# Branch merge of a hybrid attention block: seven half-size products for each pair of feature blocks, with sums on GpSimd and VectorE

## What is computed

```python
def merge_branches(o_mla, o_fox, o_mem, gates, w_br_mla, w_br_fox, w_br_mem, w_out):
    b, s = gates.shape[:2]
    y = (gates[:, :, 0] * (o_mla.reshape(b, s, -1) @ w_br_mla)
         + gates[:, :, 1] * (o_fox.reshape(b, s, -1) @ w_br_fox)
         + gates[:, :, 2] * (o_mem.reshape(b, s, -1) @ w_br_mem))
    return y @ w_out
```

## Time and profile before

| | |
|---|---|
| median of 3 runs | 1071.58 us (1070.4 to 1073.7) |
| profiled execution | 1072.0 us |
| its span, first to last instruction | 1069.8 us |
| granted TensorE clock, mean | 0.992 |
| PE busy | 1035.6 us (97%) |
| DVE busy | 597.4 us (56%) |
| ACT busy | 182.0 us (17%) |
| POOL busy | 94.7 us (9%) |

### The profile page before, as it was taken

One profiled execution on the slowest core, in us unless ns is written; L12 is line 12 of the kernel. 1 busy time (PEld: TensorE's weight loads), 2 busy tenths in 40 slices (PEclk: granted clock), 3 DMA queues, 4 the chain that ended last, 5 costly groups with the idle time before them and its releaser, 6 DMA issues.

```text
span 1069.8 us, 17897 instructions
## 1 busy us (share of the span) xinstructions
PE 1035.6 (97%) x6615; PEld 660.0 (62%) x6648; DVE 597.4 (56%) x1476; ACT 182.0 (17%) x365; POOL 94.7 (9%) x111
## 2 busy tenths in 40 slices
PE   8999999999999999998999999999999999999985
PEld 4499569989888755466655555555555555555541
DVE  2445047777666333366686655555655655654636
ACT  1411224443223100010001011011011101101102
POOL 4140000000000000002014410000000000000000
PEclk9999999999999999999999999999999999999988
DMA  9633443523767598561598999999999999999981
GB/s 335 220 117 105 131 145 112 203 95 115 280 216 248 188 335 323 245 221 43 217 412 336 406 413 419 421 420 418 420 417 412 422 420 421 421 420 419 407 346 61
DMA packets 82333, 313.56 MB, mean 293 GB/s; under 512 B 13208, under 2 KB 24016, under 8 KB 56024
## 3 DMA queue, kind: packets, MB, share of 16 engines
q1 hardware_dynamic: 64864, 276.90, 65.7%
q10 hardware_dynamic: 10128, 19.40, 5.0%
q0 software_dynamic: 7280, 16.44, 4.3%
HBM read 306.24 MB, written 11.34 MB: 297 GB/s over the span
## 4 chain that ended last, share of the span: by engine, by line
PE 93%; DVE 4%; DMA 2%; issue 1%; ACT 0%; SPq 0%; DVEq 0%
PE ps_P L1372 21%; PE ps_P L1120 16%; PE ps_V L1396 11%; PE ps_V L1360 8%; PE ps_V L1308 6%; PE ps_P L999 4%; PE ps_S L1360 4%; PE ps_V L1156 4%; PE ps_T L1354 3%; PE ps_T L992 2%; DMA arena<-w_e_gate 1%; PE ps_P L1008 1%; PE ps_P L1174 1%; PE ps_V L1342 1%; PE ps_S L1379 1%
## 5 line engine op out<-in xcount | busy, mean ns | idle before, releaser
L1372 PE MATMUL ps_P<-arena,branch_out 128*64 128x256 f32 (+1 forms) x2176 | 236.1, 385 | 4.7 <-DMA arena<-w_e_gate 3.9
L1372 PEld LDWEIGHTS ps_P<-arena,branch_out 128*64 128x64 f32 (+1 forms) x2176 | 153.2, 137 | 95.6 <-issue 25.7
L1396 PE MATMUL ps_V<-arena,branch_out 128*64 128x512 f32 (+1 forms) x544 | 120.6, 598 | 0.0
L1610 ACT ACTIVATE weight_ring<-ps_V,merge 128x512 f32<-128x512 f32 x66 | 45.3, 687 | 382.0 <-PE ps_V L1396 356.3
L1360 PE MATMUL ps_V<-weight_ring,branch_out 128*128 128x512 bf16 x363 | 93.7, 390 | 2.2
L2133 DVE TENSOR_TENSOR branch_out<-branch_out,ps_P 128x256 f32<-128x256 f32 x33 | 13.9, 421 | 143.5 <-PE ps_P L1372 143.4
L2160 DVE TENSOR_TENSOR x_sb<-x_sb,ps_V 128x512 f32<-128x512 f32 x132 | 87.4, 684 | 1.3 <-PE ps_V L1360 1.3
L2123 DVE TENSOR_TENSOR weight_ring<-weight_ring 128x512 f32<-128x512 f32 x64 | 44.4, 693 | 68.2 <-ACT weight_ring L1610 65.9
L1120 PE MATMUL ps_P<-xT,weight_ring 128*128 128x192 f32 x432 | 78.9, 327 | 0.8 <-ACT arena L1522 0.8
L1396 PEld LDWEIGHTS ps_V<-arena,branch_out 128*64 128x64 f32 (+1 forms) x544 | 34.8, 135 | 68.7 <-issue 68.6
L1120 PEld LDWEIGHTS ps_P<-xT,weight_ring 128*128 128x128 f32 x432 | 70.2, 190 | 3.3 <-issue 2.9
(11 more groups left out here) (360 smaller groups left out, 1250.8 us busy)
## 6 DMA issues: line engine op xcount, KB each, us to landing
arena<-w_e_gate SPq DMA_DIRECT2D x68, 1024.0 KB
arena<-w_e_up SPq DMA_DIRECT2D x68, 1024.0 KB
arena<-w_e_down SPq DMA_DIRECT2D x68, 1024.0 KB
weight_ring<-w_in SPq DMA_DIRECT2D x12, 1024.0 KB, 9.2
weight_ring<-w_in ACTq DMA_DIRECT2D x8, 1024.0 KB, 6.7
gates<-arena ACTq DMA_DIRECT2D x12, 384.0 KB, 3.1
arena<-fox_k_t SPq DMA_DIRECT2D x8, 512.0 KB, 3.8
arena<-cache_fox_v SPq DMA_DIRECT2D x8, 512.0 KB, 4.3
```

The lines of the kernel that those rows point to most:

```text
L1372: last = mm(bank[r:r + wide, 0:256], xgT[q][:, k, r:r + wide], w[h][:, k, :], start=(k == 0), stop=(k == KD - 1))
L1396: last = mm(ps["V"][half][r:r + wide, :], hidT[:, m, r:r + wide], ew_down[h][:, m, half * 512:(half + 1) * 512], start=(m == 0), stop=(m = ...
L1610: fn(yo[:, half * 512:(half + 1) * 512], ps["V"][half][:, :], ACT.Copy, scale=now_info[:, q, 1:2])\
```

## The change

The 24 entries of the merge become 12 units, u from 0 to 11, of the seven-product scheme that the gates already use. A unit takes a pair of feature blocks (m = 0 and 1, or 2 and 3) of one branch and one half cb, and splits the 512 features of `oT` into two halves of 256 and the 384 tokens into two of 192. A product is two matmuls on 192 columns in place of four, so that a unit has 14 matmuls where two entries had eight on 384 columns. The units are numbered on from the gates' units (`JOIN` = 18) and use the same two `ps_P` banks and the same semaphores.

- Sums of weights: three for each unit ahead of it (`sum_weights`) and one within it (a12), each 128 x 256, all on GpSimd.
- Sums of `oT`: four for each branch, 128 x 384 each, on VectorE (the entries `"mix"`). The four of branch 0 stand among the last entries of attention, the eight others behind products 2 and 4 of units 0 to 3.
- Sums of results: ScalarE copies product 0, VectorE adds the others, as in the gates' units.
- Gating: one VectorE multiplication of 128 x 768 in each unit (`gate_rows`), behind the last sum.
- Addition to `yT`: one of 128 x 768 on GpSimd (`join`) for the units of branches 1 and 2, a unit later.
- Gate tiles are loaded in pairs. The eight of the start come behind ScalarE's copy of product 0 of unit 0.
- The load of expert pair 1 also waits for the last addition to `yT`, since the new buffers lie in its place.

```diff
+    at = max(i for i, st in enumerate(s) if st[:2] == ("V", "ov")) + 1
+    for m in range(4):
+        s.insert(at + 3 * m, ("mix", 0, m))
+    sums = [("mix", br, m) for br in (1, 2) for m in range(4)]
+    for u in range(JOINS):
+        for r in range(7):
+            s.append(("W", JOIN + u, r))
+            if r in (2, 4) and sums:
+                s.append(sums.pop(0))
-    s += [("V", "b", cb, br, m) for cb, br, m in MERGE]
...
+            def sum_weights(u):
+                i = JOIN + u
+                a11, a12, a21, a22 = join_weights(u)
+                all_, less = join_sums(u)
+                n = first_of["br"] + u // 2
+                pool.wait_ge(w_loaded[n % NW], loads_of(n))
+                pool.wait_ge(done["W"], done_at("W", JOIN - 1 if u < 2 else i - 2, 4))
+                nc.gpsimd.tensor_tensor(all_, a21, a22, ALU.add).then_inc(w_mixed, 1)
+                pool.wait_ge(w_mixed, 4 * i + 1)
+                nc.gpsimd.tensor_tensor(less, all_, a11, ALU.subtract).then_inc(w_mixed, 1)
+                nc.gpsimd.tensor_tensor(a21, a11, a21, ALU.subtract).then_inc(w_mixed, 1)
+
+            def join(u):
+                cb, br, m = join_parts(u)
+                if br:
+                    pool.wait_ge(gated, u + 1)
+                    if br == 2:
+                        pool.wait_ge(merged, joined_at(cb, 1, m))
+                    nc.gpsimd.tensor_tensor(join_rows(u), join_rows(u), join_two[u % 2], ALU.add).then_inc(merged, 1)
+
+            sum_weights(0)
+            for u in range(JOINS):
...
+                pool.wait_ge(done["W"], done_at("W", i, 2))
+                pool.wait_ge(w_mixed, 4 * i + 3)
+                nc.gpsimd.tensor_tensor(a12, a12, join_sums(u)[1], ALU.subtract).then_inc(w_mixed, 1)
+                if u + 1 < JOINS:
+                    sum_weights(u + 1)
+                if u:
+                    join(u - 1)
+            join(JOINS - 1)
...
+                nk = 2 if i >= JOIN else 4
+                for k in range(nk):
+                    last = mm(gate_bank(i, r), w[:, k, :], x[:, k, :], start=(k == 0), stop=(k == nk - 1))
...
+                            act.wait_ge(done["W"], done_at(*st))
+                            fn(product_cells(i)[:, 0, 0:HALF], gate_bank(i, r), ACT.Copy).then_inc(w_copied, 1)
+                            if u == 0:
+                                make_gates(TWO - 1)
+                                while gates["stored"] < gates["made"]:
+                                    store_gates()
+                                for n in range(4, 4 + KD):
+                                    load_gate(n)
...
+            def gate_rows(u):
+                for n in (2 * u, 2 * u + 1):
+                    dve.wait_ge(gates_loaded[gate_buffer(n)], 16 * (1 if n < 4 else (n - 4) // KD + 1))
+                dve.wait_ge(w_read, 7 * (JOIN + u) + 7)
+                to = join_rows(u) if join_parts(u)[1] == 0 else join_two[u % 2]
+                V.tensor_tensor(to, join_two[u % 2], join_gates(u), ALU.mult).then_inc(gated, 1)
...
                     else:
                         dve.wait_ge(w_read, 7 * i + 5)
                         V.tensor_tensor(c12, out, c12, ALU.add).then_inc(w_read, 1)
+                        if i >= JOIN:
+                            gate_rows(i - JOIN)
...
+                    V.tensor_tensor(to, more, less, ALU.subtract).then_inc(o_mixed, 1)
```

More of the change, by code:

```diff
@@ L468, in build @@
         rs = M.take(len(U))
+        joining = Space(R_A, 18432, 12288)
+        o_mix = [[joining.take(2, HALF) for _ in range(4)] for _ in range(3)]
+        join_two = [joining.take(2, T) for _ in range(2)]
         egate = [v.rearrange("p m c -> p (m c)")[:, i * 512:i * 512 + T] for v in (fkTc[0], mkTc[0]) for i in range(2)] + [xT[:, k, :] for k in range(KD)]
```

136 lines of the change are left out of this document (87 added, 49 removed).

## The result

The changed kernel takes 1083.89 us (median of 4 runs, 1081.06 to 1084.77) against 1071.84 (1070.4 to 1073.7): ratio 1.0109, 95% interval 1.009 to 1.0129. It is 12.05 us slower; the forecast was 5.2. Its profiled execution took 1083.82 us, with a span of 1082.0 at a granted clock of 0.991.

What follows compares the result with a forecast made beforehand. PE was taken to bound the merge (62.19 of 62.20 us busy). Products 54.6, banks 5.8, burst 1.35, `oT` sums 0.2 and entry 0.47 make 62.4; serial engines add 5.0: 67.4 against 62.2, hence 1076.8 us, range 1068 to 1084.

Steps and rivals of the forecast that it cites:

- two banks: Merge products on PE: each bank comes back later than the other bank's product covers, 0.48 us a unit, 5.8 in all.
- ScalarE's burst: Start of the merge: eight gate loads ahead of unit 1's copy of product 0 delay product 2, 1.35 us once.
- sums of `oT`, held or not: VectorE in units 0 to 3: 0.2 us for too little room, 2.0 for meeting GpSimd's a12 in three units.
- gating against GpSimd's addition: Units with an addition to `yT`: gating and GpSimd's work run serially, +0.4 us in each of seven units, 2.8.
- GpSimd's price: GpSimd's additions in the merge: 2.1 ns a column, 0.64 and 1.71 us; 4.5 us a unit fits into 5.03.
- The lock: In the merge, VectorE operations with two SBUF inputs and GpSimd's additions run one after the other, 5.0 us in all.
- The entry: Before the merge's first product: a sum of `oT` ahead of VectorE's last copy moves that copy by 0.47 us.
- The exit: End of the merge: last gating and addition end about 3.4 us behind the last product, hidden before the output projection's need.
- The stage behind: The experts' stage moves as a whole with the merge's end, its first matmul staying 89.8 us behind.
- The third, GpSimd as the bound: Rival for the merge: at 2.5 to 3 ns a column GpSimd limits the units, 1082 to 1088 us; chance 0.12.
- The second, the bank in time: Rival for the merge: banks return below 0.65 us, only product 6's 0.27 stays, 1069.2 or 1066 us; chance 0.08.
- The first, no lock between additions: Rival for the merge: GpSimd's and VectorE's work lie side by side, +0.2 us, 1071.8 us; chance 0.32.

Runs made afterwards that it cites:

- e5: The changed kernel with the merge's products in four PSUM banks in turn instead of two: 1072.0 us, ratio to before 0.9993.
- e3: The changed kernel with GpSimd's additions to `yT` left out, so the output sums only branch 0: 1074.0 us (one run).
- e6: The changed kernel with ScalarE's eight gate loads issued as 2, 4 and 2 in the first three units: 1083.1 us (one run).
- e1: The changed kernel with three cell buffers instead of two for a unit's products: 1079.7 us, ratio to before 1.006.
- f2: As f1, but the addition to `yT` stays on GpSimd, ahead of the next unit's weight sums: 1077.8 us, ratio to before 1.0055.
- e8: The changed kernel with four banks and three cell buffers: 1071.5 us, ratio to before 0.999.
- e2: The changed kernel with GpSimd making the addition to `yT` ahead of the next unit's weight sums: 1081.1 us, ratio to before 1.0078.
- e4: The changed kernel with the weight sums on VectorE, GpSimd keeping only the additions to `yT`: 1079.9 us, ratio to before 1.0072.
- e7: The changed kernel with the addition to `yT` on VectorE, two banks and two cell buffers: 1082.5 us, ratio to before 1.0087.
- f1: The changed kernel with four banks, three cell buffers, gate loads spread and the addition to `yT` on VectorE: 1069.1 us, ratio to before 0.9966.
- f3: As f1, but with the changed kernel's two cell buffers: 1068.6 us, ratio to before 0.9962.
- f4: As f1, with two of the first branch's four `oT` sums moved behind attention's last copy: 1068.6 us, ratio to before 0.9963.

## Why the prediction was wrong, point by point

The direction held, and of the mechanisms two banks and one port. The size did not, and one mechanism was missing. By the prediction's own terms, with what the runs measured (apart from the products and the banks they are differences between kernels, so that their sum meets 70.9 by construction):

| term | predicted us | measured us | from |
|---|---|---|---|
| 84 products | 54.6 | 54.6 | e5, units of 4.55 |
| two banks | 5.8 | 7.8 | e3 and e5, 12 x (5.20 - 4.55) |
| ScalarE's burst | 1.35 | 0.7 | e6 |
| sums of `oT`, held or not | 0.2 + 2.0 | 2.2 | what is left of e3's 65.3 |
| gating against GpSimd's addition | 2.8 | 2.8 | e1 less e3 |
| some tenths for gating against weight sums | 0.2 | 0 | e3's timeline |
| the copy behind the addition of unit u-2 | not seen | 2.8 | changed less e1 |
| merge | 66.9, with the entry's 0.47 67.4 | 70.9, with the entry's 0.5 71.4 | |

**The step that failed** is in "GpSimd's price": "A unit with an addition to `yT` then has 4 x 0.64 + 1.71 = 4.3 us of GpSimd's, with 0.2 for its waits 4.5, and lasts 5.03. It fits." I compared a load with a period, and asked only whether the next unit's sums are ready. A load that fits says nothing of a circle. What GpSimd's last operation in the row gives free, the cell buffer, is asked for by ScalarE's copy, then product 2, and product 2 releases GpSimd's first. The circle is 6.12 us long, 4.7 in GpSimd's five operations (390.42 to 395.10) and 1.45 through the copy and product 2 (395.10 to 396.55), with every link of it known ahead: the prices were all but right. I had named who waits for the weight sums, and not who waits for the addition, except at the merge's exit. With the circle the additions cost 5.6 us (changed less e3), where the prediction had 2.8 for them.

**The two banks** were the second error, a size: 0.65 a unit and not 0.48. In the unit of e3 whose gating is shown above, products 1 to 5 start at 408.15, 408.87, 409.57, 410.30 and 410.95, and product 6 at 411.92; by 413.35, product 1 of the next unit, two more distances have passed. Less 0.65 each, that is 0.07, 0.05, 0.08, 0, 0.32, and 0.13 for the two. Product 6's 0.32 was foreseen at 0.34. The small losses, which I had at 0.07 in two places of a unit, 0.14 in all, come to 0.33, as the banks never get ahead again.

**GpSimd's price** was nearly right. The prediction took 0.64 and 1.71 us; alone, the changed kernel's operations take 0.72 and 1.81 (L981 and L990 above), which is 2.1 ns a column and 0.18 fixed: a load of 4.7 in place of 4.3. The Trainium skill ("GPSIMD Engine Reference", section Elementwise, side-by-side cycle accounting) has 4497 ns for 2048 columns, 2.2 each; by that alone 256 columns would be 0.56 and 768 1.7. The rows are above it by what is fixed.

**The lock** was there as forecast, and was the case that no row of before had shown. Two VectorE inputs in SBUF beside a GpSimd addition: the gating 0.96 alone and 1.95 behind an addition of 1.81; the sums of `oT` 0.55 and 0.91; GpSimd's sums 0.73 and 1.04. VectorE's additions with an input in PSUM stay at 0.34 to 0.36 beside the same work. By the rule of the Trainium skill ("SBUF — State Buffer", section Terms, and the reading of its diagram), whichever begins first keeps the port for its whole instruction; the trace agrees in both orders. What the rule does not tell is its price, which hangs on when the two meet: 2.8 us in e1, where an addition is late, and nothing for the gating in e3. That the 2.8 is also the forecast is luck. The prediction had seven units of 0.4 each, the two engines' work added up against PE's time; e1 has three units of 0.75 to 1.0 by a bank that comes back late, and three of 0.15. In the changed kernel itself the lock's share for the additions can't be told apart: the circle accounts for the whole of its units of 6.13, and the weight sums in them are not held (0.72).

**The sums of `oT`** were forecast at 0.65 in units 0, 2 and 3, hidden in unit 1, and 0.2 for VectorE's room. They cost about the same in another spread, some 0.5 in each of units 0 to 3: unit 1 lasts 5.67 without the burst (e6), units 2 and 3 5.73, against 5.20. How much of it is the lock and how much VectorE's own time no run separates.

**ScalarE's burst** had its mechanism right and its size double: unit 1 loses 0.7. The prediction's own figures, 8.1 less 6.6, give 1.5 and not 1.35. Counted from the merge's start, product 2 of unit 1 began at 7.7 in place of 8.1, and without the burst (e6) at 7.0 in place of 6.6, since unit 0 lasts 5.67 and not 5.03.

**The entry** was right: the sum of `oT` ahead of the last copy, a wait of 1.0 in place of 0.5, +0.5 against 0.47. **The exit** was right as well: the experts begin 524.2 - 434.4 = 89.8 us behind the merge's end, to the tenth as foreseen.

**The stage behind** did not just move. In the changed kernel PE waited there for a gather of rows, which the stage of before never did:

```profile
PE ps_T L1455 <- DMA weight_ring<-x_rows,idx: 3.4, 1, 3.4
...
PE ps_P L1473 <- DMA arena<-w_e_gate: 2.2, 1, 2.2
```

From the merge's end to the program's end it is 645.7 us in before and 647.6 here. Over all profiled executions it is 643.5 to 645.7 without that wait (before, e3, e5, f2), 645.1 with 2.1 us of it (e8), and 647.5 to 649.1 with 2.7 to 5.4 (changed, e1, e2, e4, e6, e7, f1, f3, f4). GpSimd issues the gather as long after the experts' start as before (101.5 us and 101.3), but it lands 9.9 us later in place of 5.6. What differs is the order against the load of a pair's `w_e_down` on SP's queue. In before the gather goes first, by 1.58 us:

```profile
615.23 1.06 POOL L927 DMA_INDIRECT weight_ring<-x_rows,idx  x1 [0.31 <-issue]
...
616.81 0.81 SPq L737 DMA_DIRECT2D arena<-w_e_down  x2
```

and in the changed kernel the load does, by 0.24:

```profile
625.50 0.81 SPq L790 DMA_DIRECT2D arena<-w_e_down  x2
...
625.74 1.06 POOL L1018 DMA_INDIRECT weight_ring<-x_rows,idx  x1 [0.32 <-issue]
```

All 14 profiles divide by this order: in the four without the wait the gather is 1.3 to 4.2 us ahead of the load, in the ten with it at most 0.6 ahead, or behind. That the load holds the gather up is read from the order alone; no run changed it. The load comes when PE frees its buffer, and PE was 1.6 us further on in this stage than in before (101.1 us behind the experts' start in place of 102.7). The lead arises some 45 us into the stage, where the granted clock reads 0.83 in before (553.9 to 563.9 us) and 1.00 in the changed kernel (564.2 to 574.2): of these two, the execution with the higher clock ran into the wait. The clock does not decide it alone, since e1, e4 and f4 have 0.83 at this place too, with a gather that is issued 1 to 2 us later, and wait as well. Each kernel has one profile only, so whether the change has a part in this isn't shown.

**The sum of the miss.** To the forecast's 5.2 come 2.8 of the circle and 2.0 of the banks, less 0.65 of the burst and 0.2 of the gating: 9.15, which is the merge's 8.7 and the entry's 0.5. The remaining 3.0 of the 12.2 between the two spans are the 1.1 of the program's start and the 1.9 behind the merge.

**The rivals.** The third, GpSimd as the bound at 1082 to 1088, had the time, for another reason than its own: GpSimd's rate was the one forecast, and its load was never too large in the changed kernel. The second, the bank in time, was wrong for two banks, which cost more than forecast; four banks make it true: 1072 with the additions on GpSimd, 1068.6 with them on VectorE. The first, no lock between additions, is ruled out by the gating of 1.95.

## What to carry to other kernels

When a new engine joins a loop, its load against the period is half of the question: for each buffer that it frees, follow who waits for it, what that one releases, and whether the way leads back to the engine's own queue, and then sum the circle. Halving the matmuls of a product halves the time in which its bank must be read out, so ask for more banks along with it; that also moves the waits to later products, which can stretch a circle over two units (e5) without opening it. An operation costs by where it stands: the same addition of 768 columns cost 5.6 us in all behind GpSimd's weight sums, 4.4 on VectorE with two banks (e7 against e3), and 0.1 a unit on VectorE with four (f3's units 5 to 7, 10 and 11 of 4.65 against 4.55; in units 3 and 4, where sums of `oT` fall in, f3 loses 1.4 in all).

## What the runs showed of the hardware

- VectorE (both inputs in SBUF) and GpSimd's additions exclude each other for the whole instruction, in both orders: 0.96 becomes 1.95 behind 1.81 us of GpSimd's (changed kernel), and 1.81 becomes 2.53 behind the gating (e8). The time of the one that is held includes its wait.
- GpSimd's TENSOR_TENSOR in float32: 0.72 us for 128 x 256, 1.81 for 128 x 768. VectorE's with both inputs in SBUF: 0.42 for 128 x 256, 0.96 for 128 x 768.
- A float32 product of four records on 192 columns, with four banks, comes every 0.65 us, with weights from `weight_ring` or `arena` and moving data from `branch_out` or `arena`: seven in 4.55 us (e5, f3), so that 84 would take 54.6. With two banks, where nothing else holds the unit, the same product comes every 0.74 (5.20 / 7, e3).
- A gather issued on GpSimd's queue landed after 5.6 us in before, where the next experts' load went out 1.58 us behind it, and after 9.9 in the changed kernel, where that load went out 0.24 ahead.
